# Expert tables of a large two-block layer stack: all first products ahead of the second, their results kept in DRAM, and the scatter groups set between them

## The chip, the cores and the metric

The kernel runs on one core of a Trainium2 chip. The metric is device time in microseconds from the start of the program to its end; lower is better. A core has five engines with a queue each: PE (TensorE, matmuls), ACT (ScalarE), DVE (VectorE), POOL (GpSimd) and SP (SyncE, which here only issues the loads of weights). They meet through semaphores. ACT and POOL issue some DMAs of their own.

## The reference, cut to what matters

A stack of two blocks over 256 tokens of width 1024. The change touches only the expert tables (`_peer`), which come twice, in layers 0 and 1 of the second block. A token picks 128 of 16384 experts, by product keys:

```python
q = (xt @ wq).reshape(T, PEER_HEADS, 2, PEER_DQ_HALF)
s1 = jnp.einsum('thd,nd->thn', q[:, :, 0], k1)
s2 = jnp.einsum('thd,nd->thn', q[:, :, 1], k2)
v1, i1 = lax.top_k(s1, PEER_TOPK)
v2, i2 = lax.top_k(s2, PEER_TOPK)
cand = (v1[..., :, None] + v2[..., None, :]).reshape(T, PEER_HEADS, PEER_TOPK * PEER_TOPK)
sc, pos = lax.top_k(cand, PEER_TOPK)
eidx = jnp.take_along_axis(cidx, pos, axis=-1).reshape(T, PEER_HK)
gate = jax.nn.softmax(sc.astype(jnp.float32), axis=-1)
...
act = jax.nn.gelu(jnp.einsum('td,tkd->tk', xb, ub), approximate=False)
return jnp.einsum('tk,tkd->td', gb * act, vb)
```

## The kernel before, in words

The kernel doesn't gather experts. It computes the first product of every expert with every token (the table `peer_u`, 128 tiles of 128 experts, 512 KB each), applies Gelu, multiplies by a dense table of gates `Gt` (zero where an expert wasn't chosen), and runs the second product with all of `peer_v`, again 128 tiles. Two tiles make a **pair**: 64 pairs of first products (`pe_pair`) and 64 of second products (`down_step` twice), each into one PSUM bank or into four accumulators.

Weights come in float32 and are multiplied as a high and a low part in fp32r, three matmuls for one. The two parts are made on the way: SP loads a tile into one of 3 raw buffers, ACT copies a half tile to its high part (L478), and DVE or POOL subtracts to get the low part (L501). The halves stand in a ring of 5 (`NHALF`), so that a half's place is free once PE has done the half five before it. A pair has four halves, numbered on through the program. Every engine's program calls `fed(n)` once its part of the work has used n more tiles, and splits then, in order, every half that may be split by that count:

```python
def splittable(self, m, tiles):
    if m == len(self.halves) or self.ready[self.halves[m][0]] > tiles:
        return False
    return self.freed[m] < 0 or self.halves[self.freed[m]][0] < tiles
```

Here `freed[m]` is half m - 5. `fed(2)` of pair p is called ahead of waiting for the pair's product, and counts its two tiles as used. The instructions that it writes wait, on ACT, for PE to be done with half m - 5, and on DVE and POOL for ACT's high part. Which of DVE and POOL makes the low part is written in the stream of loads (`stream_order`, `lo=`).

The gates come from the **choice** (`dve_choice`, on DVE, once for each 128 tokens: top 16 of 256 sums for 8 heads, indices, differences; `act_choice` takes Exp on ACT; then the softmax's end, three transposes on PE and a copy). The choice's results become `Gt` in the **scatter**, by groups of four tokens: for each two tokens DVE or POOL compares an iota with the second index (`p.b`: DVE for tokens 0 and 1 of a group, L95; POOL for tokens 2 and 3, L100), DVE compares with the first and multiplies by the gate (`p.a`, L100, one operation a token), PE multiplies the two for each token (128x128, fp32), and ACT copies four tokens' result to `Gt` (L155). The factors stand in three buffers of two tokens each.

The order is written out by hand, alike on all engines: 16 query tiles with their top 16; pairs 0 to 9; choice 0; scatter of tokens 0 to 127; pairs 10 to 17; choice 1; scatter of tokens 128 to 255; then a mixed run, in which first products 18 to 63 and second products of all pairs alternate. The Gelu results of pairs 0 to 17 are spilled to DRAM (`act_early`, four buffers) and read back on POOL's queue into three buffers `hb`; those of the later pairs go straight into `hb`. In the mixed run DVE multiplies `hb` by the gates (1.05 us at 512 elements, `p.hg`), ACT takes the high part (`p.hh`) and DVE the low part (`p.hl`), for PE's second product. The spill's four buffers lie in `arena`, the second products' left factors in `hid`.

Of the kernel before, what the change touches and what calls it, by code (L numbers as in the profile page):

```python
# [24 lines left out]
NSPILL = 18  # L25
# [179 lines left out]
def stream_order(dram):  # L205
# [27 lines left out]
    def peer(layer):  # L233
        for i in range(16):
            put(dram["wq"][layer, i])
        for i in range(2 * NSPILL):
            put(dram["peer_u"][layer, i])
        for k, n in steps(64, 3):
            i = turns()[n]
            if k == 0 and i >= NSPILL:  # L240
                for j in range(2):
                    put(dram["peer_u"][layer, 2 * i + j], lo="dve")
            elif k == 2:
                for j in range(2):
                    put(dram["peer_v"][layer, 2 * i + j], lo="dve")
# [42 lines left out]
def turns():  # L288
    return [x for i in range(NSPILL) for x in (i, NSPILL + i)] + list(range(2 * NSPILL, 64))


class Shared:


    def __init__(self, nc, ctx, dram, out):
# [27 lines left out]
        self.spill = nc.dram_tensor("spill", (2, NSPILL, 128, 512), F32)  # L323
# [1928 lines left out]
class Peer:  # L2252
    def __init__(self, S, layer):
# [16 lines left out]
        self.sel = R.get(3, 128)  # L2270
        self.gs = R.get(16)
        self.kT2 = R.get(2, 128)
        self.rb = [R.get(512) for _ in range(4)]
# [6 lines left out]
        self.turns = turns()  # L2280
        self.norm_in, self.norm_out = 5 + 2 * layer, 6 + 2 * layer

    def pe(self, pe):
# [23 lines left out]
        for k, i in steps(64, 3):  # L2307
            if k == 0:
                if self.turns[i] >= NSPILL:
                    self.pe_pair(pe, self.turns[i])  # L2310
            elif k == 2:
                h = self.hs[i % 2]
                pe.wait_ge(S.acted, "p.hh", n, i)
                pe.wait_ge(S.vdone, "p.hl", n, i)
                for j in range(2):
                    pe.down_step(lambda t: (h[:, 256 * j + 128 * t:256 * j + 128 * t + 128],
                                            h[:, 512 + 256 * j + 128 * t:640 + 256 * j + 128 * t]),
                                 (i, j) == (0, 0), (i, j) == (63, 1))
                S.product.at["p.down", n, i] = S.product.n
# [9 lines left out]
    def pe_choice(self, pe, t):  # L2329
        S, n = self.S, self.layer  # L2330
        b = pe.open("p.c", n, t)
        pe.wait_ge(S.vdone, "p.sel", n, t)
        for a in range(3):
            ins = pe.tr(b[:, 128 * a:128 * a + 128], self.sel[:, a, :])
        pe.out(ins, ("p.c", n, t))
# [12 lines left out]
    def act(self, act):  # L2348
# [10 lines left out]
        for i in range(10):  # L2359
            self.act_early(act, i)  # L2360
        self.act_choice(act, 0)
        for t0 in range(0, 128, 4):
            self.act_scatter(act, t0)
        for i in range(10, NSPILL):
            self.act_early(act, i)
        self.act_choice(act, 1)
        act.wait_ge(S.vdone, "p.iT", n, 1)
        for i in range(4):
            act.wait_ge(S.load(f"spill{n}_{i}"), "spill", NSPILL - 1 - (NSPILL - 1 - i) % 4)
        for t0 in range(128, 256, 4):  # L2370
            self.act_scatter(act, t0)
        for k, i in steps(64, 3):
            if k == 0:
                p = self.turns[i]
                if p >= NSPILL:
                    act.fed(2)
                    act.wait_ge(S.product, "p.u", n, p)
                    if i >= 3:
                        act.wait_ge(S.vdone, "p.hl", n, i - 3)
                    act.act(self.hb[i % 3], S.bank["p.u", n, p], ACT.Gelu, ("p.ge", n, i), ("drained", ("p.u", n, p)))  # L2380
            elif k == 1:
# [12 lines left out]
    def act_early(self, act, i):  # L2394
        S, n = self.S, self.layer
        r = self.rb[i % 4]
        ring = S.load(f"spill{n}_{i % 4}")
        act.fed(2)
        act.wait_ge(S.product, "p.u", n, i)
        if i >= 4:  # L2400
            act.wait_ge(ring, "spill", i - 4)
# [4 lines left out]
    def act_choice(self, act, t):  # L2406
        S, n = self.S, self.layer
        g3 = self.sel[:, 2, :].rearrange("p (h k) -> p h k", h=8)
        act.wait_ge(S.vdone, "p.g", n, t)
        act.act(g3, g3, ACT.Exp, ("p.g", n, t))  # L2410

# [6 lines left out]
    def dve(self, dve):  # L2418
# [12 lines left out]
        dve.fed(20)  # L2431
        self.dve_choice(dve, 0)
        for t0 in range(0, 128, 4):
            self.dve_scatter(dve, t0)
        dve.fed(2 * NSPILL - 20)
        self.dve_choice(dve, 1)
        for t0 in range(128, 256, 4):
            self.dve_scatter(dve, t0)
        for k, i in steps(64, 3):
            if k == 0:  # L2440
                p = self.turns[i]
                r3 = self.hb[i % 3].rearrange("p (i t) -> p i t", i=2)
                g = self.Gt[:, :, 2 * p:2 * p + 2].rearrange("p t i -> p i t")
                if p < NSPILL:
                    dve.wait_ge(S.load(f"back{n}_{i % 3}"), "back", i)
                else:
                    dve.fed(2)
                    dve.wait_ge(S.acted, "p.ge", n, i)
                dve.wait_ge(S.acted, "p.G", n, 252)
                dve.tt(r3, r3, g, ALU.mult, ("p.hg", n, i))  # L2450
# [30 lines left out]
    def dve_choice(self, dve, t):  # L2481
        S, n = self.S, self.layer
        iota16 = S.C["iota"][:, 0:16]
        VV, II, IIf, SC, PP, oh, sel, gs = self.VV[t], self.II[t], self.IIf, self.SC, self.PP, self.oh, self.sel, self.gs
# [20 lines left out]
        dve.tt(g3, SC, bc(SC[:, :, 0], 2, 16), ALU.subtract, ("p.g", n, t))  # L2505
        dve.wait_ge(S.acted, "p.g", n, t)
# [3 lines left out]
        dve.wait_ge(S.product, "p.c", n, t)  # L2510
        dve.cp(self.iT[:, :, 128 * t:128 * t + 128], S.bank["p.c", n, t][:, 0:384].rearrange("p (a t) -> p a t", a=3),
               ("p.iT", n, t), ("drained", ("p.c", n, t)))

    def dve_scatter(self, dve, t0):
        S, n = self.S, self.layer
        iota, iT = S.C["iota"], self.iT
        for tp in (0, 2):
            m = t0 + tp
            ab = self.AB[m // 2 % 3]
            dve.wait_ge(dve.done, "p.iT", n, t0 // 128)  # L2520
# [9 lines left out]
    def pool(self, pool):  # L2530
        S, n = self.S, self.layer
        pool.fed(16 + 20)
        for t0 in range(0, 128, 4):
            self.pool_scatter(pool, t0)
        pool.fed(2 * NSPILL - 20)
        for t0 in range(128, 256, 4):
            self.pool_scatter(pool, t0)
        for k, i in steps(64, 3):
            if k == 0:
                p = self.turns[i]  # L2540
                if p < NSPILL:
                    pool.wait_ge(S.load(f"spill{n}_{p % 4}"), "spill", p)
                    if i >= 3:
                        pool.wait_ge(S.vdone, "p.hl", n, i - 3)
                    else:
                        pool.wait_ge(S.acted, "p.G", n, 252)
# [5 lines left out]
            elif k == 2:  # L2552
                pool.fed(2)
# [229 lines left out]
```

## Time and profile before

| | us |
|---|---|
| median of 3 runs | 3538.53 (3537.34 to 3541.25) |
| the profiled execution | 3538.66 |
| its span, first to last instruction | 3536.7 |
| PE busy | 3163.5 (89% of the span) |
| DVE busy | 2315.6 (65%) |
| ACT busy | 1856.4 (52%) |
| POOL busy | 813.2 (23%) |
| mean granted TensorE clock | 0.925 |

Busy time is summed over an engine's instructions; it doesn't tell whether the engine was waited for. The granted clock is 1.00 at 2.4 GHz and 0.50 at 1.2 GHz. The two expert-table stages run from about 1465 to 2397 us and from about 2591 us to the end.

### The profile page before, as it was taken

What the parts mean: (1) busy time and instruction counts of PE and PEld (TensorE: products, weight loads), DVE (VectorE), ACT (ScalarE), POOL (GpSimd) and SP (SyncE); (2) the same over time, 40 slices, a digit from 0 to 9 for tenths busy, and PEclk for the clock granted to TensorE, in tenths of its full rate; (3) what the DMA queues carried; (4) which work ended last, traced back from release to release, by engine and by line L of the source; (5) the groups of instructions that cost most, each with busy time, mean ns of one, the idle gap of its engine ahead of it and who ended that gap; (6) DMA issues with size and microseconds to landing.
All of it is one profiled execution on the core that took longest, in us unless ns stands there. A gap on an engine that the chain in (4) does not pass through costs nothing.

```text
span 3536.7 us, 48626 instructions
## 1 busy us (share of the span) xinstructions
PE 3163.5 (89%) x17902; PEld 2733.0 (77%) x17902; DVE 2315.6 (65%) x4081; ACT 1856.4 (52%) x2816; POOL 813.2 (23%) x770
## 2 busy tenths in 40 slices
PE   7769999887999968889499999997798769999998
PEld 6658888656788856788488899996588758889997
DVE  0558998125899946585966666664668486666666
ACT  4447887334688834444255555554344425555554
POOL 6230000412100024588410000004368640000000
PEclk8879999788999978899799999997799979999999
DMA  5238998343799922363056666663244306666665
GB/s 184 60 125 311 370 369 325 111 143 123 275 371 371 370 69 89 117 189 91 29 163 205 211 190 188 187 186 127 64 151 149 120 20 196 210 201 190 188 188 166
DMA packets 183198, 653.75 MB, mean 185 GB/s; under 512 B 20689, under 2 KB 21073, under 8 KB 182547
## 3 DMA queue, kind: packets, MB, share of 16 engines
q1 hardware_dynamic: 170784, 617.69, 52.5%
q10 hardware_dynamic: 7476, 17.24, 1.4%
q0 software_dynamic: 4704, 15.73, 1.2%
q8 instruction: 144, 2.36, 0.3%
q14 instruction: 90, 0.74, 0.1%
HBM read 635.89 MB, written 14.68 MB: 184 GB/s over the span
## 4 chain that ended last, share of the span: by engine, by line
PE 82%; DVE 9%; ACT 3%; POOL 2%; DMA 2%; issue 1%; ACTq 0%; DVEq 0%; SPq 0%; POOLq 0%
PE ps L549 81%; DVE arena L95 3%; POOL splitb L501 2%; PE ps L560 2%; DVE hrow L105 1%; DVE arena L105 1%; ACT arena L155 1%; DMA rawb<-in_peer_u 1%; ACT splitb L478 1%; ACT L155 1%; DVE arena L100 1%; DVE arena L150 0%; DMA rawb<-in_cmp_w 0%; DVE arena L115 0%; DVE arena L145 0%
## 5 line engine op out<-in xcount | busy, mean ns | idle before, releaser
L478 ACT ACTIVATE splitb<-rawb 128x512 fp32r<-128x512 f32 x1328 | 833.7, 630 | 1006.9 <-PE ps L549 900.5
L549 PE MATMUL ps<-hH,splitb 128*128 128x256 f32 x5248 | 982.6, 286 | 7.3 <-POOL splitb L501 7.0
L501 POOL TENSOR_TENSOR splitb<-rawb,splitb 128x512 fp32r<-128x512 f32 x448 | 598.5, 1349 | 1605.0 <-ACT splitb L478 1595.0
L501 DVE TENSOR_TENSOR splitb<-rawb,splitb 128x512 fp32r<-128x512 f32 x880 | 596.7, 691 | 499.2 <-ACT splitb L478 498.8
L549 PEld LDWEIGHTS ps<-hH,splitb 128*128 128x128 f32 x5248 | 839.3, 194 | 14.7 <-issue 4.4
L549 PE MATMUL ps<-splitb,hid 128*128 128x512 f32 x3444 | 810.7, 392 | 9.2 <-ACT hid L155 9.2
L549 PEld LDWEIGHTS ps<-splitb,hid 128*128 128x128 f32 x3444 | 644.5, 189 | 141.1 <-ACT hid L155 9.6
L549 PE MATMUL ps<-hL,splitb 128*128 128x256 f32 x2624 | 749.1, 285 | 0.0
L549 PEld LDWEIGHTS ps<-hL,splitb 128*128 128x128 f32 x2624 | 510.4, 195 | 3.5
L549 PE MATMUL ps<-experts_r 128*128 128x512 f32 (+1 forms) x1348 | 332.1, 397 | 15.3 <-ACT experts_r L155 9.0
L549 PEld LDWEIGHTS ps<-experts_r 128*128 128x128 f32 x1348 | 253.7, 194 | 70.6 <-ACT experts_r L155 7.5
L155 ACT ACTIVATE arena<-ps 128x512 f32<-128x512 f32 (+4 forms) x328 | 173.5, 529 | 199.7 <-PE ps L549 181.2
L501 DVE TENSOR_TENSOR splitb<-experts,splitb 128x1024 fp32r<-128x1024 f32 x188 | 228.1, 1224 | 17.1 <-ACT splitb L478 13.5
L478 ACT ACTIVATE splitb<-experts 128x1024 fp32r<-128x1024 f32 x192 | 202.0, 1060 | 46.2 <-PE ps L549 46.0
L549 PE MATMUL ps<-splitb,hH 128*128 128x512 f32 x640 | 215.9, 420 | 10.3 <-ACT arena L155 9.6
L549 PE MATMUL ps<-arena 128*128 128x128 f32 (+8 forms) x896 | 179.5, 353 | 37.8 <-ACT arena L155 14.4
L549 PE MATMUL ps<-splitb,experts_r 128*128 128x512 f32 x780 | 196.1, 396 | 0.0
L549 PE MATMUL ps<-aux 128*128 128x128 f32 x1024 | 177.2, 310 | 20.9 <-DVE aux L100 6.0
L100 POOL TENSOR_SCALAR aux<-cst,aux 128x128 f32<-128x128 f32 x256 | 165.3, 656 | 126.5 <-DVE aux L111 99.6
L549 PEld LDWEIGHTS ps<-arena 128*128 128x128 f32 (+3 forms) x896 | 134.4, 227 | 77.2 <-issue 24.6
L549 PEld LDWEIGHTS ps<-aux 128*128 128x128 f32 x1024 | 142.3, 205 | 56.7 <-issue 36.2
L501 DVE TENSOR_TENSOR experts_r<-experts,experts_r 128x1024 fp32r<-128x1024 f32 x140 | 169.8, 1224 | 22.4 <-ACT experts_r L478 17.5
(147 smaller groups left out, 3245.2 us busy)
## 6 DMA issues: line engine op xcount, KB each, us to landing
rawb<-in_peer_u SPq DMA_DIRECT2D x256, 512.0 KB, 4.1
rawb<-in_peer_v SPq DMA_DIRECT2D x256, 512.0 KB, 4.1
experts<-in_moe_gu SPq DMA_DIRECT2D x228, 512.0 KB, 5.4
experts<-in_moe_d SPq DMA_DIRECT2D x108, 512.0 KB, 5.3
rawb<-in_moe_gu SPq DMA_DIRECT2D x92, 512.0 KB, 5.4
rawb<-in_moe_d SPq DMA_DIRECT2D x52, 512.0 KB, 5.3
rawb<-in_wq SPq DMA_DIRECT2D x32, 512.0 KB, 3.6
spill<-arena ACTq DMA_DIRECT2D x36, 256.0 KB, 4.2
```

The source lines that it names most:

```text
L95: self.eng.tensor_tensor(o, a, b, op).then_inc(self.done.sem, self.done.step(*names))
L100: self.eng.tensor_scalar(o, a, s1, s2, op0, op1).then_inc(self.done.sem, self.done.step(*names))
L105: self.eng.scalar_tensor_tensor(out=o, in0=a, scalar=s, in1=b, op0=op0, op1=op1, accum_out=accum).then_inc(self.done.sem, self.done.step(* ...
L155: self.eng.activation(o, a, f, bias=bias, scale=scale).then_inc(self.done.sem, self.done.step(*names))
L478: self.eng.activation(S.split(m)[0], S.raw(n)[:, off:off + w], ACT.Copy).then_inc(S.hi.sem, S.hi.step(("half", m)))
L501: self.eng.tensor_tensor(l, raw, h.bitcast(F32), ALU.subtract).then_inc(self.low.sem, self.low.step(("half", m), *([("raw", n)] if last el ...
L549: return self.eng.matmul(o, w, x, start=start, stop=stop)
L560: return self.eng.transpose(o, a, self.S.ident)
```

## The change: what it does

All 64 first products run first and all are spilled, through two buffers that now lie in `gb` (the second half of `hid`'s place). Both choices stand on DVE ahead of its first `fed`, with the softmax's end parted off (`dve_gates`) and each with its own `sel`; ACT takes the Exps behind pairs 17 and 21 and copies the transposed choices (`act_places`) behind pair 22. The scatter's 64 groups follow pairs 23 to 58 (`groups(p)`), two behind 28 of them and one behind 8. Of the low parts of `peer_u`, POOL makes all up to pair 23 and those of odd pairs behind it, DVE those of even pairs from 24 on. The second products come last in one run, each reading its spilled result back. Nothing is computed differently.

```diff
+        for i in range(128):
+            put(dram["peer_u"][layer, i], lo="dve" if i // 2 >= SCATTER and i // 2 % 2 == 0 else "pool")
+        for i in range(128):
+            put(dram["peer_v"][layer, i], lo="dve")
...
+CHOICE = 22
+SCATTER, SCATTERED = 23, 59
+
+
+def groups(p):
+
+    first, last = (min(64, max(0, 64 * (i - SCATTER) // (SCATTERED - SCATTER))) for i in (p, p + 1))
+    return [4 * g for g in range(first, last)]
...
-        self.rb = [R.get(512) for _ in range(4)]
+        self.rb = [S.gb[:, 1024 + 512 * i:1536 + 512 * i] for i in range(2)]
...
     def pe(self, pe):
-        for i in range(10):
-            self.pe_pair(pe, i)
-        self.pe_choice(pe, 0)
-        for t0 in range(0, 128, 4):
-            self.pe_scatter(pe, t0)
-        for i in range(10, NSPILL):
-            self.pe_pair(pe, i)
-        self.pe_choice(pe, 1)
-        for t0 in range(128, 256, 4):
-            self.pe_scatter(pe, t0)
...
+        for p in range(64):
+            self.pe_pair(pe, p)
+            if p == CHOICE:
+                for t in range(2):
+                    self.pe_choice(pe, t)
+            for t0 in groups(p):
+                self.pe_scatter(pe, t0)
+        for i in range(64):
+            h = self.hs[i % 2]
+            pe.wait_ge(S.acted, "p.hh", n, i)
+            pe.wait_ge(S.vdone, "p.hl", n, i)
...
     def act(self, act):
+        for p in range(64):
+            self.act_early(act, p)
+            if p == CHOICE - 5:
+                self.act_choice(act, 0)
+            elif p == CHOICE - 1:
+                self.act_choice(act, 1)
+            elif p == CHOICE:
+                for t in range(2):
+                    self.act_places(act, t)
+            for t0 in groups(p):
+                self.act_scatter(act, t0)
+        for p, i in steps(64, 2):
+            if p == 0:
...
+                if i == 1:
+                    for k in range(2):
+                        act.wait_ge(S.load(f"spill{n}_{k}"), "spill", 62 + k)
...
     def dve(self, dve):
-        dve.fed(20)
-        self.dve_choice(dve, 0)
-        for t0 in range(0, 128, 4):
-            self.dve_scatter(dve, t0)
-        dve.fed(2 * NSPILL - 20)
-        self.dve_choice(dve, 1)
-        for t0 in range(128, 256, 4):
-            self.dve_scatter(dve, t0)
+        for t in range(2):
+            self.dve_choice(dve, t)
+        for t in range(2):
+            self.dve_gates(dve, t)
+        for p in range(64):
+            dve.fed(2)
+            for t0 in groups(p):
+                self.dve_scatter(dve, t0)
...
     def pool(self, pool):
+        pool.fed(16)
+        for p in range(64):
+            pool.fed(2)
+            for t0 in groups(p):
+                self.pool_scatter(pool, t0)
+        for i in range(64):
+            pool.wait_ge(S.load(f"spill{n}_{i % 2}"), "spill", i)
+            if i >= 3:
+                pool.wait_ge(S.vdone, "p.hl", n, i - 3)
+            else:
+                pool.wait_ge(S.acted, "p.G", n, 252)
+            ring = S.load(f"back{n}_{i % 3}")
+            pool.eng.dma_start(self.hb[i % 3], S.spill.ap()[n, i, :, :]).then_inc(ring.sem, ring.step(("back", i)))
+        pool.fed(128)
```

How it moves the instructions is seen in their order on DVE and POOL, the two engines that the scatter's matmuls wait for. On DVE before, in the scatter of layer 0 (`aux<-cst,aux` are the comparisons, 128x256 for two tokens' second index, 128x128 for one token's first index and gate), groups of four tokens follow each other with nothing between:

```order
L95 TENSOR_TENSOR aux<-cst,aux 128x256 [waits s_product]
L100 TENSOR_SCALAR aux<-cst,aux 128x128 x2
L100 TENSOR_SCALAR aux<-cst,aux 128x128 [waits s_product]
L100 TENSOR_SCALAR aux<-cst,aux 128x128
L95 TENSOR_TENSOR aux<-cst,aux 128x256 [waits s_product]
```

On DVE now, behind pairs 25 and 26 of layer 0 (`splitb<-rawb,splitb` are the low parts of halves, `s_hi` is ACT's high part):

```order
L500 TENSOR_TENSOR splitb<-rawb,splitb 128x512 [waits s_hi] x3
L94 TENSOR_TENSOR aux<-cst,aux 128x256 [waits s_product]
L99 TENSOR_SCALAR aux<-cst,aux 128x128 x2
L99 TENSOR_SCALAR aux<-cst,aux 128x128 [waits s_product]
L99 TENSOR_SCALAR aux<-cst,aux 128x128
L94 TENSOR_TENSOR aux<-cst,aux 128x256 [waits s_product]
L99 TENSOR_SCALAR aux<-cst,aux 128x128 x2
L99 TENSOR_SCALAR aux<-cst,aux 128x128 [waits s_product]
L99 TENSOR_SCALAR aux<-cst,aux 128x128
L500 TENSOR_TENSOR splitb<-rawb,splitb 128x512 [waits s_hi]
L94 TENSOR_TENSOR aux<-cst,aux 128x256 [waits s_product]
```

Three low parts (the last three halves of pair 26) stand ahead of the groups behind pair 25, and one (the first half of pair 28) ahead of those behind pair 26. On POOL before, a run of low parts ends with that of the first half of pair 11, and the comparisons for tokens 2 and 3 of each group of the first scatter follow:

```order
L501 TENSOR_TENSOR splitb<-rawb,splitb 128x512 [waits s_hi] x133
L100 TENSOR_SCALAR aux<-cst,aux 128x128 [waits s_vdone]
L100 TENSOR_SCALAR aux<-cst,aux 128x128
L100 TENSOR_SCALAR aux<-cst,aux 128x128 [waits s_product]
L100 TENSOR_SCALAR aux<-cst,aux 128x128
```

On POOL now, behind pairs further on in the same layer, one behind an odd pair first, and then an even one:

```order
L500 TENSOR_TENSOR splitb<-rawb,splitb 128x512 [waits s_hi]
L99 TENSOR_SCALAR aux<-cst,aux 128x128 [waits s_product]
L99 TENSOR_SCALAR aux<-cst,aux 128x128
L99 TENSOR_SCALAR aux<-cst,aux 128x128 [waits s_product]
L99 TENSOR_SCALAR aux<-cst,aux 128x128
L500 TENSOR_TENSOR splitb<-rawb,splitb 128x512 [waits s_hi] x3
L99 TENSOR_SCALAR aux<-cst,aux 128x128 [waits s_product]
L99 TENSOR_SCALAR aux<-cst,aux 128x128
```

POOL has the other parity: one low part ahead of the groups behind an odd pair, three ahead of those behind an even one.

## Rows read from the trace of the kernel before

**Rows 1.** The page, part 4: the chain that ended last, in shares.

```profile
PE 82%; DVE 9%; ACT 3%; POOL 2%; DMA 2%; issue 1%; ACTq 0%; DVEq 0%; SPq 0%; POOLq 0%
```

**Rows 2.** Layer 0, stretches: us, busy PE, PEld, DVE, ACT, POOL, clock, DMA, GB/s.

```profile
1522.22:1584.20 61.98, 58.48 (x483) 57.78 (x481) 57.07 (x143) 30.68 (x50) 56.62 (x37) 1.00 0.62 194
1584.20:1592.03 7.83, 0.90 (x5) 0.54 (x4) 2.22 (x7) 2.71 (x4) 4.86 (x5) 0.72 0.64 208
1592.03:1639.86 47.83, 43.89 (x257) 35.43 (x257) 46.84 (x158) 18.52 (x31) 40.71 (x64) 0.94 0.01 1
1639.86:1686.10 46.24, 46.24 (x387) 46.10 (x385) 2.75 (x4) 24.89 (x40) 34.65 (x27) 1.00 0.70 207
1686.10:1728.34 42.24, 0.94 (x4) 0.53 (x4) 38.36 (x86) 2.71 (x4) 0.82 (x2) 0.55 0.07 24
1728.34:1776.12 47.78, 43.84 (x256) 35.52 (x257) 46.80 (x158) 18.52 (x31) 40.49 (x64) 0.94 0.00 1
1776.12:1786.73 10.61, 6.00 (x52) 5.82 (x50) 5.25 (x8) 6.27 (x9) 1.15 (x2) 0.95 0.44 136
1786.73:2396.00 609.27, 609.27 (x3689) 547.93 (x3690) 394.36 (x556) 326.62 (x538) 8.62 (x16) 1.00 0.63 194
```

**Rows 3.** The same columns, layer 1, the wait for choice 1.

```profile
2812.61:2855.18 42.57, 0.88 (x4) 0.53 (x4) 38.34 (x85) 2.71 (x4) 0.81 (x2) 0.55 0.08 27
```

**Rows 4.** Timeline, PE: start, duration, form, count, idle before with its releaser.

```profile
1479.25 1.38 PE L549 MATMUL ps<-arena 128*128 128x128 f32 x10 [0.39 <-ACT arena L155]
...
1786.73 8.38 PE L549 MATMUL ps<-splitb,hid 128*128 128x512 f32 x24 [4.61 <-ACT hid L155]
```

**Rows 5.** Timeline, POOL: low halves, and comparisons of the scatter.

```profile
1531.98 31.40 POOL L501 TENSOR_TENSOR splitb<-rawb,splitb 128x512 fp32r<-128x512 f32 x23 [1.66 <-ACT splitb L478]
1563.88 24.37 POOL L501 TENSOR_TENSOR splitb<-rawb,splitb 128x512 fp32r<-128x512 f32 x13 [0.49 <-ACT splitb L478]
...
1638.04 1.29 POOL L100 TENSOR_SCALAR aux<-cst,aux 128x128 f32<-128x128 f32 x2 [0.19 <-PE ps L549]
```

**Rows 6.** Timeline: end of a pair on PE; ACT's splits; DVE's halves.

```profile
1781.83 0.28 PE L549 MATMUL ps<-hH,splitb 128*128 128x256 f32 x1
...
1782.21 0.63 ACT L478 ACTIVATE splitb<-rawb 128x512 fp32r<-128x512 f32 x1 [0.86 <-PE ps L549]
...
1798.08 0.63 ACT L478 ACTIVATE splitb<-rawb 128x512 fp32r<-128x512 f32 x1 [0.87 <-PE ps L549]
...
1781.58 2.49 DVE L501 TENSOR_TENSOR splitb<-rawb,splitb 128x512 fp32r<-128x512 f32 x4
1784.78 1.05 DVE L95 TENSOR_TENSOR aux<-aux,arena 128x512 f32<-128x512 f32 x1 [0.72 <-ACT aux L155]
...
1798.75 0.69 DVE L501 TENSOR_TENSOR splitb<-rawb,splitb 128x512 fp32r<-128x512 f32 x1 [0.81 <-ACT splitb L478]
```

**Rows 7.** Timeline, DVE and PE: first group of a scatter, and last.

```profile
1591.15 0.42 DVE L95 TENSOR_TENSOR aux<-cst,aux 128x256 f32<-128x256 f32 x1
...
1592.03 7.32 PE L549 MATMUL ps<-aux 128*128 128x128 f32 x36 [1.51 <-DVE aux L100]
...
1774.14 0.41 DVE L95 TENSOR_TENSOR aux<-cst,aux 128x256 f32<-128x256 f32 x1
...
1776.12 0.36 PE L549 MATMUL ps<-hH,splitb 128*128 128x256 f32 x1
```

**Rows 8.** Stretches, columns as in rows 2: the clock and PE.

```profile
1570.00:1584.00 14.00, 10.52 (x84) 10.21 (x84) 12.05 (x5) 4.55 (x8) 14.00 (x9) 1.00 0.51 160
...
1390.00:1393.00 3.00, 1.53 (x12) 1.18 (x10) 2.72 (x5) 0.70 (x2) 0.00 (x0) 1.00 0.33 134
1393.00:1400.00 7.00, 6.94 (x20) 5.33 (x20) 6.15 (x15) 0.63 (x1) 0.71 (x1) 0.51 0.01 2
...
1786.00:1792.00 6.00, 5.27 (x13) 4.14 (x14) 3.06 (x4) 1.12 (x2) 0.54 (x1) 0.50 0.30 105
```

**Rows 9.** The spill tensor's DMAs, issue to landing.

```profile
DMA to landing us min/median/max: 2.0/4.3/6.1
```

More of the change, by code:

```diff
@@ L24 @@
 EXPERT_ROOM = 1024 * XRAW + 2560
-NSPILL = 18
 AB_AUX = dict(conv=32, gateb=8, headg=512, rel=8, wif=64)
@@ L2269, in __init__ @@
         self.oh = R.get(8, 16, 16)
-        self.sel = R.get(3, 128)
+        self.sel = [R.get(3, 128) for _ in range(2)]
         self.gs = R.get(16)
         self.kT2 = R.get(2, 128)
-        self.rb = [R.get(512) for _ in range(4)]
+        self.rb = [S.gb[:, 1024 + 512 * i:1536 + 512 * i] for i in range(2)]
         self.iT = S.aux[:, 0:768].rearrange("p (a t) -> p a t", a=3)
@@ L2296, in pe @@
                 pe.out(ins, ("p.s", n, t, i0))
-        for i in range(10):
-            self.pe_pair(pe, i)
-        self.pe_choice(pe, 0)
-        for t0 in range(0, 128, 4):
-            self.pe_scatter(pe, t0)
-        for i in range(10, NSPILL):
-            self.pe_pair(pe, i)
-        self.pe_choice(pe, 1)
-        for t0 in range(128, 256, 4):
-            self.pe_scatter(pe, t0)
[L2307 to L2319, printed above, removed]
+        for p in range(64):
[9 more added lines that the diff above has]
+            pe.wait_ge(S.vdone, "p.hl", n, i)
+            for j in range(2):
+                pe.down_step(lambda t: (h[:, 256 * j + 128 * t:256 * j + 128 * t + 128],
+                                        h[:, 512 + 256 * j + 128 * t:640 + 256 * j + 128 * t]),
+                             (i, j) == (0, 0), (i, j) == (63, 1))
+            S.product.at["p.down", n, i] = S.product.n
         S.product.at["rows", self.norm_out] = S.product.n
@@ L2395, in act_early @@
         S, n = self.S, self.layer
-        r = self.rb[i % 4]
-        ring = S.load(f"spill{n}_{i % 4}")
+        r = self.rb[i % 2]
+        ring = S.load(f"spill{n}_{i % 2}")
         act.fed(2)
         act.wait_ge(S.product, "p.u", n, i)
-        if i >= 4:
-            act.wait_ge(ring, "spill", i - 4)
+        if i >= 2:
+            act.wait_ge(ring, "spill", i - 2)
         act.act(r, S.bank["p.u", n, i], ACT.Gelu, ("p.ue", n, i), ("drained", ("p.u", n, i)))
@@ L2407, in act_choice, with act_places @@
         S, n = self.S, self.layer
-        g3 = self.sel[:, 2, :].rearrange("p (h k) -> p h k", h=8)
+        g3 = self.sel[t][:, 2, :].rearrange("p (h k) -> p h k", h=8)
         act.wait_ge(S.vdone, "p.g", n, t)
         act.act(g3, g3, ACT.Exp, ("p.g", n, t))
+    def act_places(self, act, t):
+        S, n = self.S, self.layer
+        act.wait_ge(S.product, "p.c", n, t)
+        act.cp(self.iT[:, :, 128 * t:128 * t + 128], S.bank["p.c", n, t][:, 0:384].rearrange("p (a t) -> p a t", a=3),
+               ("p.iT", n, t), ("drained", ("p.c", n, t)))
     def act_scatter(self, act, t0):
@@ L2531, in pool @@
         S, n = self.S, self.layer
[L2532 to L2546, printed above, removed]
-                    ring = S.load(f"back{n}_{i % 3}")
-                    pool.eng.dma_start(self.hb[i % 3], S.spill.ap()[n, p, :, :]).then_inc(
-                        ring.sem, ring.step(("back", i)))
-                else:
-                    pool.fed(2)
-            elif k == 2:
-                pool.fed(2)
+        pool.fed(16)
[12 more added lines that the diff above has]
+        pool.fed(128)
     def pool_scatter(self, pool, t0):
```

64 lines of the change are left out of this document (10 added, 54 removed).

## The prediction, made before the changed kernel was run

> **What bounds the kernel now.** I read the chain that ended last first: PE holds 82% of it and DVE 9% [rows 1], so only work that PE does, or waits for, counts. Then I cut the expert-table stage of layer 0 into stretches [rows 2]. PE is busy throughout the long mixed stretch (609.27 of 609.27 us) and while it runs pairs 10 to 17 (46.24 of 46.24, so 5.78 us a pair); what it loses, it loses around the choices and the scatter. In order:
>
> - pairs 0 to 9: 61.98 us, 4.2 more than ten times 5.78;
> - the wait for choice 0: 7.83;
> - scatter of 128 tokens: 47.83, in which DVE is busy for 46.84 and sets the pace;
> - after pair 17 the wait for choice 1: 42.24, of which DVE works 38.36 and PE 0.94;
> - scatter again: 47.78;
> - one pair and a wait of 4.61 for the first down product: 10.61.
>
> Layer 1 repeats this (42.57 for the second wait) [rows 3], so I count every term twice.
>
> **What the change removes.** The two waits and the two solid scatter stretches: 7.83 + 47.83 + 42.24 + 47.78 = 145.7 us a layer. If nothing came back, that would be 291 us. The pairs and the down products remain: 64 of each, at 5.78 and, from the mixed stretch, (609.27 - 45 x 5.78 - 2.9 of slow clock) / 64 = 5.4 us.
>
> **What comes back, term 1: both choices under pairs.** Choice 0 already ran under pairs. While it did, POOL made 13 low halves in 24.37 us, 1.87 each, against 31.40/23 = 1.365 just before [rows 5]; PE eats one in 1.445. So 24.37 - 13 x 1.445 = 5.6 us of supply was lost, 4.2 of which PE felt, the rest lay in the buffers. Now a second full choice runs there with POOL still doing every low half, and POOL's margin of 0.08 a half refills almost nothing between them: 2 x 5.6 - 4.2 = 7.0 more a layer. Bounds: 4 (the same as now) to 12. By the rows POOL itself lost 24.37 - 13 x 1.365 = 6.6 us to the choice. The Trainium skill (SBUF — State Buffer, "Who interferes with whom") has a stricter rule: a DVE operation with two SBUF inputs blocks GpSimd's reads for the whole instruction. By it POOL would lose the full length of each such operation in a choice, more than the rows show; the measurement decides, and the sum keeps 7.0. Both choices' transposes stay on PE: three are the 0.94 us of PE's work in the wait [rows 2], six 1.9, or 1.8 at full clock.
>
> **Term 2: the scatter between pairs, and what stands ahead of it.** 64 groups of four tokens go behind pairs 23 to 58: two groups behind 28 of these 36 pairs, one behind 8, evenly over odd and even ones. A splitter's ring holds five halves, a pair has four. So the `fed(2)` of pair p runs up to the first half of pair p+2, and that half's buffer is freed only by the last matmul of pair p itself. `fed(2)` stands ahead of the groups on DVE and on POOL; the order shows it. Nothing for PE's scatter matmuls behind pair p can begin, on the engine that owns this fifth half, before pair p has ended. Let E be the moment at which PE could start its next matmul: 1781.83 + 0.12. ACT's split begins at 1782.21, E + 0.26; the low part begins 0.67 behind a split (1798.75 against 1798.08), at E + 0.93 [rows 6].
>
> *Behind an even pair* the fifth half is DVE's: 2.49/4 = 0.62 [rows 6], so its scatter starts at E + 1.55. The first matmul comes 0.88 later (1592.03 against 1591.15), a group takes 1.48 (47.78/32 = 1.49), and from the last group's start to the next pair it is 1.98 (1776.12 against 1774.14) [rows 7]. Two groups: 1.55 + 1.48 + 1.98 = 5.01 us until the next pair; one: 3.53.
>
> *Behind an odd pair* it is POOL's, 1.365 long: POOL is free at E + 2.30, and its two comparisons for tokens 2 and 3 take 1.29 [rows 5], to E + 3.59. PE waits for them in order, with tokens 4 to 7 behind; with 0.2 to the matmul and half a microsecond for two tokens, one group ends at 4.28; the second group's comparisons take 1.29 more, 5.57.
>
> Sum: 14 x 5.01 + 4 x 3.53 + 14 x 5.57 + 4 x 4.28 = 179.4 us a layer. PE's own part is small: ten records of the same matmul shape take 1.38 [rows 4], two records to a token, 0.28; eight tokens are 2.2 us. The rest of each 5 us is waiting, now paid 36 times. This is the step on which the forecast rests.
>
> **Term 3: the clock.** PE will be idle or thinly used for about 5 us after each pair. The granted clock fell to half after the 4.61 us wait: it was 0.50 over 1786 to 1792, and the first 24 down matmuls took 8.38 us instead of 5.4, 2.9 lost [rows 4, 8]. It also fell after 1390 to 1393, where PE was busy 1.53 of 3.00 us, and was 0.51 over the next seven. It held at 1.00 over 1570 to 1584, where gaps up to 1.62 us stood between dense halves (10.52 busy of 14.00) [rows 8]. The new stretches have 3 us of standing in 5, so I place them with the first two. A fall costs nothing while PE waits anyway; the part on dense matmuls costs. Bounds per stretch 0 and 2.9; I take 1.2, since the lower clock begins inside the wait and covers about half a pair of dense work. 36 x 1.2 = 43.2 a layer. The Trainium skill (TensorE: Matmul & The Clock Gate, "A second HAM failure mode: psum-queue depth-cycling") says that frequent short idles between groups of matmuls make the clock alternate. By that rule term 3 is paid everywhere; by the row of 1570 to 1584 it is nothing, and the sum would be 86 us less.
>
> **What I cost at nothing, and its cover.** 46 more spills a layer, written and read, 256 KB each: ACT's issue and Gelu fit in a pair (ACT is busy 24.89 of 46.24) [rows 2]; the two-buffer ring waits for the spill two pairs back, 11.5 us, and a spill's DMA lands in 4.3 us, 6.1 at most [rows 9]. Read back, three buffers give about 7.5 us between the freeing of one and its use, again against 4.3 plus 0.5 of issue; if it took over 8, every down pair would wait for it. Bytes: 1.25 MB per 5.4 us is 243 GB/s; at 207 the DMA engines are busy 0.70 of the time [rows 2], so about 0.82 then. ACT switches between Exp and Gelu four times a layer, for which no row here has a price; the halves are split five ahead, 7.2 us of cover. In the down run DVE has four low halves at 0.69, a multiplication at 1.05 and one more low part at 0.69 [rows 6], 4.5 us of work per 5.4. The first down product waits as now (4.61 and the slow clock behind): DVE must finish the fifth half, two multiplications and one low part behind pair 63; no change. ACT's wait for the last spills falls under down product 0.
>
> **Sum.** Per layer -145.7 + 7.0 + 1.8 + 179.4 + 43.2 = +85.7; twice +171. The profiled execution took 3538.66 us (span 3536.7), the median of the runs is 3538.53, so one base serves: 3710.
>
> **Rivals.**
>
> *A, the forecast:* waits and clock falls, 3710, chance 0.50.
>
> *B, waits only:* the clock holds, because dense pairs stand between: 3538.7 + 2 x 42.5 = 3624, chance 0.28. For it speaks the row of 1570 to 1584; against it the length of the standing.
>
> *C, the scatter hides (faster):* DVE and POOL prepare the tokens during the pair, so PE pays only 256 x 0.28 = 71 us: -145.7 + 71 + 8.8 = -66 a layer, 3407. For it: DVE is busy for only 2.75 of 46.24 us under pairs 10 to 17 [rows 2], so there is room for the 95 us of scatter. It decides if the 36 stretches average under (145.7 - 8.8)/36 = 3.8 us, clock included; mine are 5.0 and 1.2. Against it stand the in-order queues. Chance 0.11.
>
> *D, worse than A:* each fall costs the full 2.9: +104 instead of +43 a layer, 3832, chance 0.08. About no change (stretches of 3.8): 0.03.
>
> **How the numbers follow.** Predicted is A. The range 3590 to 3800 takes in B with its own spread (term 1 down to 4, stretches 0.3 shorter: 30 less) and A with clock losses up to 2.4; that holds 0.8. C and D lie outside. A measurement of this kernel tells about 0.2% (7 us) from no change; faster 0.11, within 0.03, slower 0.86.
>
> **What would show it.** Pairs 0 to 22 should run dense but for some 11 us of gaps that POOL ends. Choices end before pair 22, and the 42 us gap is gone. From pair 23 PE should stand after every pair: about 2.4 us until DVE's first token behind even ones, about 2 us in the middle of the first group behind odd ones, ended by POOL. The stage's stretches between pairs should average 5.0 us at full clock, about 6.2 with the falls. The granted clock should alternate there. The down run should be solid at 5.4 us. I am wrong if DVE's or POOL's scatter is found running before the pair ends (then C), or if the down run is starved by read-backs (above 8 us to land).

## The result, and the profile after

The changed kernel takes 3705.4 us (median of 4, 3698.2 to 3711.0) against 3537.9 (median of 4): 1.047 times the time before, 95% interval 1.045 to 1.049. The profiled execution took 3698.2 us. The forecast was 3710, in a range of 3590 to 3800. The page of the changed kernel (span; busy and share of it; PE's granted clock by slices; the chain, which answers to [rows 1]):

```profile
span 3696.3 us, 48810 instructions
PE 3236.9 (88%) x17902; PEld 2818.2 (76%) x17902; DVE 2211.8 (60%) x3869; ACT 1853.8 (50%) x2820; POOL 1161.1 (31%) x1070
...
PEclk9789998797999888998888899997899988889999
...
PE 79%; DVE 8%; POOL 6%; ACT 3%; DMA 2%; issue 2%; ACTq 0%; DVEq 0%; SPq 0%; POOLq 0%
```

POOL's share of the chain rose from 2% to 6%, and the clock row has 88888 and 8888 in the two places where groups stand between pairs. Layer 0 by stretches, in the columns of [rows 2]: pairs 0 to 22; the 36 stretches behind pairs 23 to 58 with the 35 pairs between them; pairs 59 to 63; the run of second products:

```profile
1522.18:1664.70 142.52, 134.04 (x1106) 132.81 (x1105) 103.68 (x226) 72.05 (x120) 132.01 (x89) 1.00 0.66 204
1671.26:2095.73 424.47, 330.68 (x2195) 317.29 (x2193) 157.28 (x392) 145.14 (x242) 182.33 (x200) 0.86 0.36 112
2095.73:2124.75 29.02, 29.02 (x243) 28.82 (x241) 7.62 (x11) 14.55 (x24) 11.95 (x11) 1.00 0.64 197
2129.20:2475.00 345.80, 345.80 (x1519) 286.11 (x1520) 268.90 (x376) 191.60 (x314) 32.80 (x61) 1.00 0.72 237
```

Only the second row loses time. With its 35 pairs at 5.78 it holds 424.5 - 202.3 = 222.2 us that isn't first products, where the forecast had 179.4 + 43.2 = 222.6; at a granted clock of 0.86. The two waits for a choice and the two blocks of scatter that the change removed are gone (145.7 a layer), and this stands in their place. The down run is solid, 345.8/64 = 5.40 us a pair.

Now PE in the middle of that row, behind pair 28 and then behind pair 29 (timeline of PE; start, duration, form, count, idle before and who ended it):

```profile
1729.83 0.28 PE L548 MATMUL ps<-hH,splitb 128*128 128x256 f32 x1
1732.32 1.20 PE L548 MATMUL ps<-aux 128*128 128x128 f32 x8 [2.21 <-DVE aux L99]
1733.73 2.01 PE L548 MATMUL ps<-aux 128*128 128x128 f32 x8 [0.22 <-DVE aux L99]
1735.39 0.56 PE L548 MATMUL ps<-hH,splitb 128*128 128x256 f32 x1
...
1742.87 0.68 PE L548 MATMUL ps<-aux 128*128 128x128 f32 x4 [0.70 <-DVE aux L99]
1745.82 1.99 PE L548 MATMUL ps<-aux 128*128 128x128 f32 x12 [2.27 <-POOL aux L99]
1747.46 0.56 PE L548 MATMUL ps<-hH,splitb 128*128 128x256 f32 x1
```

Behind the even pair PE stands 2.37 us from the moment at which it could go on (1729.95) to the first token; behind the odd one it gets two tokens, and then stands 2.27 for POOL. What DVE, POOL and ACT do at the same time, in the same columns:

```profile
1730.20 0.63 ACT L477 ACTIVATE splitb<-rawb 128x512 fp32r<-128x512 f32 x1 [0.86 <-PE ps L548]
...
1730.87 0.71 DVE L500 TENSOR_TENSOR splitb<-rawb,splitb 128x512 fp32r<-128x512 f32 x1 [9.83 <-ACT splitb L477]
1731.50 0.41 DVE L94 TENSOR_TENSOR aux<-cst,aux 128x256 f32<-128x256 f32 x1
...
1742.98 1.38 POOL L500 TENSOR_TENSOR splitb<-rawb,splitb 128x512 fp32r<-128x512 f32 x1 [8.66 <-ACT splitb L477]
1744.34 2.58 POOL L99 TENSOR_SCALAR aux<-cst,aux 128x128 f32<-128x128 f32 x4
```

DVE had been idle for 9.83 us, through the whole of pair 28, before a single low part whose high part ACT could make only behind the pair's end, and the scatter came behind it. POOL had been idle for 8.66 us, and its comparisons came behind the same kind of half.

### The profile page after: what moved, and what is told of

It reads as the page before. It is cut to its first block, busy times and chain, and to the rows that moved or that the text cites. A ratio compares the mean times of both kernels' runs of the same rounds, so it can differ in the third digit from the quotient of the medians.

```text
span 3696.3 us, 48810 instructions
## 1 busy us (share of the span) xinstructions
PE 3236.9 (88%) x17902; PEld 2818.2 (76%) x17902; DVE 2211.8 (60%) x3869; ACT 1853.8 (50%) x2820; POOL 1161.1 (31%) x1070
## 4 chain that ended last, share of the span: by engine, by line
PE 79%; DVE 8%; POOL 6%; ACT 3%; DMA 2%; issue 2%; ACTq 0%; DVEq 0%; SPq 0%; POOLq 0%
PE ps L548 77%; POOL splitb L500 5%; ACT splitb L477 2%; DVE arena L94 2%; PE ps L559 2%; POOL aux L99 1%; DVE hrow L104 1%; DVE arena L104 1%; DMA rawb<-in_peer_u 1%; DVE splitb L500 1%; ACT arena L154 1%; DVE arena L99 0%; DVE aux L99 0%; DVE aux L94 0%; DMA rawb<-in_cmp_w 0%
## 5 line engine op out<-in xcount | busy, mean ns | idle before, releaser
L500 POOL TENSOR_TENSOR splitb<-rawb,splitb 128x512 fp32r<-128x512 f32 x656 | 886.1, 1366 | 1759.0 <-ACT splitb L477 1747.2
L548 PE MATMUL ps<-hH,splitb 128*128 128x256 f32 x5248 | 1039.4, 297 | 17.4 <-POOL splitb L500 16.1
L548 PEld LDWEIGHTS ps<-hH,splitb 128*128 128x128 f32 x5248 | 885.0, 205 | 22.7 <-ACT splitb L477 13.8
L500 DVE TENSOR_TENSOR splitb<-rawb,splitb 128x512 fp32r<-128x512 f32 x672 | 454.6, 692 | 726.2 <-ACT splitb L477 725.8
L548 PE MATMUL ps<-hL,splitb 128*128 128x256 f32 x2624 | 772.3, 294 | 0.0
L548 PEld LDWEIGHTS ps<-hL,splitb 128*128 128x128 f32 x2624 | 537.7, 205 | 0.0
L548 PE MATMUL ps<-aux 128*128 128x128 f32 x1024 | 207.7, 364 | 186.9 <-DVE aux L99 109.2
L548 PEld LDWEIGHTS ps<-aux 128*128 128x128 f32 x1024 | 176.1, 253 | 213.6 <-POOL aux L99 88.8
L154 ACT ACTIVATE arena<-ps 128x512 f32<-128x512 f32 (+3 forms) x292 | 152.5, 522 | 345.4 <-PE ps L548 335.6
L2528 POOL DMA_DIRECT2D aux<-spill x128 | 68.9, 539 | 604.7 <-DVE hid L94 581.4
```

Source lines behind the costliest of these rows:

```text
L154: self.eng.activation(o, a, f, bias=bias, scale=scale).then_inc(self.done.sem, self.done.step(*names))
L500: self.eng.tensor_tensor(l, raw, h.bitcast(F32), ALU.subtract).then_inc(self.low.sem, self.low.step(("half", m), *([("raw", n)] if last el ...
L548: return self.eng.matmul(o, w, x, start=start, stop=stop)
L2528: pool.eng.dma_start(self.hb[i % 3], S.spill.ap()[n, i, :, :]).then_inc(ring.sem, ring.step(("back", i)))
```

## The experiments

Each kernel is the changed one with the edit shown. Times are medians in us; the kernel before took 3536 to 3538 beside them. "Region" is the window of layer 0 that holds the groups.

**1. The fifth half behind the groups (e1_hold1), the fourth and fifth (e2_hold2), three (e9_hold3).** A splitter can now stop short of what the count allows:

```diff
-    def fed(self, n=1):
+    def fed(self, n=1, hold=0):
         self.tile += n
-        self.split_to(self.tile)
+        last = self.half
+        while self.S.splittable(last, self.tile):
+            last += 1
+        while self.half < last - hold:
+            self.split_half(self.half)
+            self.half += 1
...
-            dve.fed(2)
+            dve.fed(2, hold=1 if groups(p) else 0)
...
-            pool.fed(2)
+            pool.fed(2, hold=1 if groups(p) else 0)
```

> The changed kernel, but behind pairs 23 to 58 DVE and POOL make the low part of the fifth half (4p+8) after the groups instead of ahead of them. Theory F (the fifth half, freed only by the pair's last matmul, stands ahead of the scatter): behind even pairs POOL's low part of half 4p+7 now ends last (about 0.75 us behind the pair), its comparisons 1.3 later, so two groups take about 4.2 us; behind odd pairs DVE is free about 0.1 behind the pair, two groups take about 3.6. Stretches sum to about 127 us a layer instead of 192, clock loss about halves: near 3550. Rival P (DVE and POOL slow each other, or PE pays for changing between the two kinds of matmul): the order of one half doesn't matter, within 20 us of 3705.

> As the one before, with the fourth and the fifth half (4p+7, 4p+8) both made after the groups. Theory F: both engines can prepare six tokens while the pair runs; PE goes on at once, two groups take about 2.9 us, one 1.3, together 92 us a layer; the clock stays at 1.00 there, and the 45 us a layer of clock loss go too: 3705 - 2 x (225 - 92) = 3440, below the kernel before. Rival P: within 20 us of 3705. Rival C (the clock falls anyway since the scatter's matmuls are thin): stretches shrink but pairs stay at 6.7 us, near 3500.

> The pair-by-pair run with three halves made after the groups instead of two (3457.5 us). Theory F: with two held back nothing of the halves is in the way any more; what is left in a double stretch (2.84 and 3.41 us) is the ring of three factor buffers, which this doesn't touch: within 10 us of 3457. Rival H (more holding back goes on helping): under 3440; if the late halves instead come too late for the next pair: over 3480.

Measured: 3529.7 with one half held back (0.998 of the kernel before, 0.997 to 0.999), 3457.5 with two (0.978, 0.976 to 0.980), 3455.5 with three (0.977, 0.975 to 0.978). Against the expectations the first is 20 us faster, the second 18 slower. The same instructions in another order are worth 248 us. The regions with one and with two:

```profile
1671.49:2010.20 338.71, 287.00 (x2194) 272.96 (x2193) 167.65 (x392) 145.46 (x243) 174.35 (x200) 0.97 0.46 141
```

```profile
1665.82:1966.74 300.92, 271.05 (x2195) 262.27 (x2193) 161.38 (x391) 144.77 (x242) 187.34 (x198) 1.00 0.50 157
```

From 424.5 to 338.7 to 300.9, and the clock from 0.86 to 0.97 to 1.00. Theory F holds, and rival P, that the order doesn't matter, falls; so does C, that the clock falls anyway. With two held back, PE goes on at once with three quarters of a double stretch and then waits for POOL, whose comparisons wait for PE to be done with a factor buffer (PE's timeline in that kernel, then POOL's):

```profile
1784.25 1.52 PE L553 MATMUL ps<-aux 128*128 128x128 f32 x12
1787.19 0.71 PE L553 MATMUL ps<-aux 128*128 128x128 f32 x4 [1.42 <-POOL aux L99]
...
1784.95 2.18 POOL L99 TENSOR_SCALAR aux<-cst,aux 128x128 f32<-128x128 f32 x2 [4.21 <-PE ps L553]
```

The ring of factor buffers isn't all of this wait. The two comparisons of POOL in that window (ns: shortest, median, longest) took 0.66 and 1.54 us. During the second, from 1785.65 to 1786.66, DVE subtracted a half and then compared for two tokens; in the changed kernel, with no such operation of DVE beside them, the last three of POOL's four comparisons above took 0.60 each.

```profile
L99 POOL TENSOR_SCALAR aux<-cst,aux x2: 662/1100/1537, 1785.0 to 1785.6; 128x128 f32<-128x128 f32 x2
```

The third half held back changes nothing (2.0 us, inside the spread of both). That fits a wait that the halves' order doesn't touch, but it doesn't part the ring from the slowed comparison.

**2. All groups in one block (e3_solid).**

```diff
-    first, last = (min(64, max(0, 64 * (i - SCATTER) // (SCATTERED - SCATTER))) for i in (p, p + 1))
-    return [4 * g for g in range(first, last)]
+    return [4 * g for g in range(64)] if p == 63 else []
```

> The changed kernel with all 64 groups in one block behind pair 63 instead of between pairs; low parts are made by the same engines as in the changed kernel. Theory F: nothing stands between groups, so 256 tokens take twice 47.8 us as before the change plus 2 to 3 us at the start, and pairs 23 to 63 run dense: 225 us of stretches and slow pairs a layer become about 99, near 3455. Rival S (the spills, the read-backs or both choices under pairs are what costs): they are all still there, so the time stays above 3650.

Measured: 3457.6 (0.978, 0.976 to 0.979). The spills, the read-backs, both choices under pairs and the owners of the low parts are all still in it, and it is 248 us faster than the changed kernel. So none of those is what costs: rival S falls. PE's timeline has one wait at the block's start, and a longer one at its end than before the change:

```profile
1901.98 5.36 PE L547 MATMUL ps<-aux 128*128 128x128 f32 x28 [2.59 <-DVE aux L99]
...
1910.43 86.42 PE L547 MATMUL ps<-aux 128*128 128x128 f32 x468 [0.21 <-POOL aux L99]
2004.09 6.29 PE L547 MATMUL ps<-splitb,hid 128*128 128x512 f32 x17 [7.25 <-ACT hid L154]
```

**3. PE's waits filled with matmuls (e4_filler).** The product that they write is overwritten by the tokens' own; the result is unchanged.

```diff
         b = pe.open("p.G", n, t0)
+        p = next(q for q in range(64) if t0 in groups(q))
         for tp in (0, 2):
             ab = self.AB[(t0 + tp) // 2 % 3]
+            fill = {(0, 0): 17, (1, 0): 6, (1, 2): 16}.get((p % 2, tp), 0) if t0 == groups(p)[0] else 0
+            for k in range(fill):
+                pe.mm(b[:, 128 * tp:128 * tp + 256], S.hH[:, k % 8, 0:128], S.hH[:, k % 8, :], True, True)
```

> The changed kernel with matmuls added whose result is overwritten: 17 of 256 columns (about 2.0 us) ahead of the first token behind even pairs, 6 ahead of the first and 16 ahead of the third behind odd pairs, to fill PE's waits and nothing else. Clock theory (term 3: low clock costs about 45 us a layer): the granted clock stays at 1.00 in the region, pairs go from 6.7 back to 5.8 us and the tokens speed up: about 3615 to 3635. Rival N (the clock costs nothing, what is lost is waiting alone): 3705 or a little more, since more matmuls are issued.

Measured: 3625.7 (1.026, 1.024 to 1.027), 79.7 us faster with some 700 more matmuls a layer. A stretch of 6 us on PE in the changed kernel (start and end, length, busy time and records of PE, granted clock, DMA share, GB/s) and two dense matmuls in it, then both here, then the whole region with all engines, in the columns of [rows 2]:

```profile
1746.00:1752.00 6.00, 6.00 (x37) 0.72 0.01 3
...
1748.03 0.63 PE L548 MATMUL ps<-hH,splitb 128*128 128x256 f32 x2
```

```profile
1746.00:1752.00 6.00, 5.60 (x45) 1.00 0.34 125
...
1750.22 0.40 PE L548 MATMUL ps<-hH,splitb 128*128 128x256 f32 x2
```

```profile
1678.15:2060.14 381.99, 366.22 (x2896) 349.96 (x2895) 157.86 (x392) 145.55 (x243) 182.03 (x200) 1.00 0.41 125
```

The changed kernel had PE busy for the whole of these 6 us with 37 records, this one gets through 45. The two stretches don't hold the same mix of matmuls; the dense ones by themselves took 0.63 us for two behind the group, and take 0.40 at full clock. The region at clock 1.00 is 382.0: less 35 x 5.78, 179.7 us of waits and tokens, where term 2 said 179.4. The rest, 424.5 - 382.0 = 42.5, is the clock, where term 3 said 43.2. Rival N falls, and the split of the loss into waiting and clock is measured.

**4. One group a tile (e5_tile), and the same without holding back (e8_tile_nohold).** Groups behind each of the tiles 46 to 109, counts tile by tile, on ACT too:

```diff
+def group_of(q):
+    return [4 * (q - 46)] if 46 <= q < 110 else []
...
             for j in range(2):
                 pe.proj(b[:, 256 * j:256 * j + 256], ("p.u", n, p))
+                for t0 in group_of(2 * p + j):
+                    self.pe_scatter(pe, t0)
...
-        for p in range(64):
-            dve.fed(2)
-            for t0 in groups(p):
+        for q in range(128):
+            dve.fed(1, hold=2 if group_of(q) else 0)
+            for t0 in group_of(q):
                 self.dve_scatter(dve, t0)
```

> Built on the run that makes the fourth and fifth half after the groups (3457.5 us): one group behind each of the 64 tiles of pairs 23 to 54 instead of two behind most pairs, splitting counted tile by tile, the last two halves that a count allows made after the group. There a double group takes 2.84 or 3.41 us and a single one 0.80 or 1.07, since tokens 6 and 7 wait for a factor buffer (three buffers of two tokens). Theory F: every stretch is a single one with its four tokens ready: 64 x 0.8 to 1.1 = 51 to 70 us a layer against 96.7, so 3404 to 3365 less nothing: about 3390. Rival Q (POOL, with 1.365 a half and 1.29 a group, becomes the bound in odd pairs: 4.0 us a tile against 3.8): 3430 to 3460.

> The tile-by-tile run (3374.8 us) with only its order of halves undone: every half that the count allows is made ahead of the group. Theory F: each of the 64 groups a layer waits again for a half that the tile just done has freed; where DVE owns it a single group takes 3.5 us, where POOL owns it 4.3, 250 us a layer instead of 52 at full clock, and with one wait for every 2.9 us of dense work the clock is low for much of the region: from 3770 (no clock loss) to 3950, likely 3850, slower than the changed kernel. Rival G (what made that run fast is the single groups, and the order of halves is worth little): under 3500.

Measured: 3374.8 with the hold (0.955, 0.954 to 0.956), 15 below the expectation and the best kernel here, 163 us faster than before the change and 331 faster than the changed kernel. Without the hold, 3911.5 (1.106, 1.104 to 1.109): in this arrangement 537 us hang on where up to two halves stand in two queues. Rival G falls. Rival Q falls too: POOL keeps up. The region with the hold, PE's timeline in it, and then two waits without the hold:

```profile
1670.42:1907.69 237.27, 237.27 (x2019) 237.27 (x2018) 170.67 (x378) 132.22 (x221) 177.82 (x190) 1.00 0.55 175
```

```profile
1741.16 1.05 PE L558 MATMUL ps<-aux 128*128 128x128 f32 x8
1744.92 1.05 PE L558 MATMUL ps<-aux 128*128 128x128 f32 x8
```

```profile
1803.94 0.71 PE L558 MATMUL ps<-aux 128*128 128x128 f32 x4 [2.27 <-POOL aux L99]
1812.29 1.22 PE L558 MATMUL ps<-aux 128*128 128x128 f32 x4 [2.83 <-POOL aux L99]
```

With the hold PE is busy for all 237.27 us from behind the first group on, a tile and its group come every 3.76 us (1744.92 - 1741.16), and a group costs 3.76 - 2.89 = 0.87 us, 0.22 a token. Without it the expectation of 3850 was 61 us short; it had left 40 us a layer for the clock. Over the whole region of layer 0 the granted clock is 0.80:

```profile
1664.44:2175.10 510.66, 345.44 (x2025) 330.74 (x2025) 147.98 (x384) 134.70 (x225) 166.28 (x192) 0.80 0.26 83
```

Less 63 tiles at 2.89, that leaves 328.6 us, 79 more than the 250 expected at full clock. The slower clock is the likely place of it; no run fills these waits to show it.

**5. All low parts on DVE (e6_dvelow).**

```diff
-            put(dram["peer_u"][layer, i], lo="dve" if i // 2 >= SCATTER and i // 2 % 2 == 0 else "pool")
+            put(dram["peer_u"][layer, i], lo="dve" if i // 2 > SCATTER else "pool")
```

> The changed kernel with the low parts of all pairs from 24 on made by DVE, POOL keeping only its comparisons. Theory F: the fifth half is DVE's behind every pair, so every stretch is like those behind even ones: first token after 2.37 us, never a wait for POOL in the middle; at full clock 28 x 5.01 + 8 x 3.53 = 168.5 instead of 179.4 us a layer, clock losses about as before: 3680 to 3690, still far above 3538. Rival P (POOL and DVE on one port is what slows the region): without POOL's subtractions the stretches fall well under 4 us, and the time comes near 3600.

Measured: 3637.7 (1.028, 1.027 to 1.030). Both expectations missed it, theory F's by 42 to 52 us and rival P's by 38. The waits came as theory F has them, also behind the odd pair 29 (the second row of PE's timeline; behind it the region in the columns of [rows 2]):

```profile
1735.92 1.20 PE L548 MATMUL ps<-aux 128*128 128x128 f32 x8 [2.19 <-DVE aux L99]
1746.63 1.20 PE L548 MATMUL ps<-aux 128*128 128x128 f32 x8 [2.19 <-DVE aux L99]
```

```profile
1676.90:2067.89 390.99, 305.44 (x2194) 291.18 (x2193) 188.67 (x462) 144.16 (x240) 76.02 (x126) 0.93 0.37 122
```

The region at 391.0 holds 188.7 us beside its pairs against 222.2. Term 2's change of owner accounts for 179.4 - 168.5 = 10.9 of the 33.5; the clock, 0.93 against 0.86, goes with the rest. What I had wrong was "clock losses about as before": with one wait of 2.35 us behind every pair and then tokens without a gap, the clock mostly holds. It isn't the odd pairs' wait in the middle alone that brings it down in the changed kernel. There a stretch and the pair behind it had the same clock behind pair 28 and behind pair 29:

```profile
1730.11:1742.17 12.06, 9.63 (x64) 9.30 (x64) 5.67 (x15) 4.21 (x7) 3.42 (x5) 0.86 0.35 107
1742.17:1754.94 12.77, 9.80 (x65) 9.25 (x64) 3.70 (x10) 4.21 (x7) 7.21 (x8) 0.87 0.31 92
```

Which property of the gaps costs the clock is open. Rival P's 3600 isn't reached: the waits are as long as F says, though POOL makes no low parts there. Its reason, that the two engines slow each other, is seen, but not on the path that PE waits for (last section).

**6. The second choice's four large lookups left out (e7_nohot).** The second 128 tokens get wrong experts.

```diff
+            if t == 0:
-            dve.tt(oh, bc(pf, 3, 16), i16, ALU.is_equal)
-            dve.tt(oh, oh, bc(i4[:, :, side, :], 2, 16), ALU.mult)
+                dve.tt(oh, bc(pf, 3, 16), i16, ALU.is_equal)
+                dve.tt(oh, oh, bc(i4[:, :, side, :], 2, 16), ALU.mult)
```

> The changed kernel with the four 128x2048 comparisons and multiplications of the second choice left out (its one-hot lookup isn't computed, so the second 128 tokens get wrong experts). Term 1: pairs 0 to 22 took 142.5 us, 9.6 more than 23 x 5.78; these four operations slow POOL's low parts, so the second cluster of gaps (4.5 us ending near 1626) mostly goes and the stretch takes about 138 us. Rival: the gaps come from the loads of tiles, and stay at 142.

PE's longest gaps within pairs 0 to 22 of the changed kernel come in two clusters, one for each choice:

```profile
1577.37 0.36 PE L548 MATMUL ps<-hH,splitb 128*128 128x256 f32 x1 [1.23 <-POOL splitb L500]
1580.64 0.35 PE L548 MATMUL ps<-hH,splitb 128*128 128x256 f32 x1 [1.60 <-POOL splitb L500]
...
1616.86 0.36 PE L548 MATMUL ps<-hH,splitb 128*128 128x256 f32 x1 [1.62 <-POOL splitb L500]
1622.63 0.35 PE L548 MATMUL ps<-hH,splitb 128*128 128x256 f32 x1 [1.22 <-POOL splitb L500]
1625.91 0.36 PE L548 MATMUL ps<-hH,splitb 128*128 128x256 f32 x1 [1.62 <-POOL splitb L500]
```

Without the four operations the first cluster stands and the second is gone; pairs 0 to 22 take 137.8 us instead of 142.5, where about 138 was expected. The whole program took 3691.2 us, 7.0 less than the profiled execution of the changed kernel (one execution each):

```profile
1523.82:1661.62 137.80, 133.50 (x1108) 132.80 (x1107) 92.33 (x222) 72.35 (x120) 124.51 (x89) 1.00 0.67 214
```

So the gaps are POOL's low parts slowed by these operations on DVE, not late loads. Two of these operations in the changed kernel (DVE's timeline), and POOL's six low parts around the four (ns: shortest, median, longest):

```profile
1609.99 2.29 DVE L94 TENSOR_TENSOR arena<-arena,cst 128x2048 f32<-128x2048 f32 x1
1612.32 3.27 DVE L94 TENSOR_TENSOR arena<-arena 128x2048 f32<-128x2048 f32 x1
...
L500 POOL TENSOR_TENSOR splitb<-rawb,splitb x6: 1289/3200/3319, 1610.3 to 1622.5; 128x512 fp32r<-128x512 f32 x6
```

Four of the six took 3.1 to 3.3 us and two 1.29, so each of the four lost about 2.0; and of DVE's operations three took 3.2 to 3.4 instead of 2.29. The Trainium skill (SBUF — State Buffer, "Who interferes with whom") names the pair, DVE operations with two SBUF inputs against GpSimd's reads, and calls it an exclusive lock. The trace agrees: each engine loses nearly the other's whole operation (2.0 of 2.29 us, 1.0 of 1.29).

## Why the prediction was right, step by step

- **Removed, 145.7 us a layer.** Right: no wait for a choice is left, and no solid block of scatter.
- **Term 1, both choices under pairs, +7.0.** Pairs 0 to 22 lost 142.5 - 23 x 5.78 = 9.6; with the 4.2 of before taken off, +5.4. The place and the cause are shown by experiment 6. The prediction took the loss as an average of 6.6 us a choice and read it as milder than one engine blocking the other for a whole operation; taken one by one, the low parts that meet such an operation do lose nearly all of it. Transposes: 1.8 forecast; 1671.26 - 1664.70 less a pair of 5.78 leaves 0.8.
- **Term 2, waits between pairs, +179.4.** Right to 0.3 us at full clock (179.7 in experiment 3), and by its parts: there the stretch behind pair 28 is 4.91 us (1738.59 - 1733.68) and the one behind pair 29 is 5.47 (1749.90 - 1744.43), against 5.01 and 5.57 forecast. PE's first token came 2.37 us behind an even pair (2.43 forecast). The cause, a half that the pair itself frees standing ahead of the groups on DVE and on POOL, is shown from both sides: holding halves back removes it (experiment 1), splitting finer without holding back multiplies it (experiment 4).
- **Term 3, the clock, +43.2.** 42.5 in the trace, 39.9 a layer by the medians ((3705.4 - 3625.7)/2). The size was chosen between bounds of 0 and 2.9 a stretch, so that it fits this closely is partly luck; experiment 5 shows that I did not know which shape of gap brings the clock down. The Trainium skill's sentence on short idles between groups of matmuls (TensorE: Matmul & The Clock Gate, "A second HAM failure mode: psum-queue depth-cycling") fits the changed kernel, where the granted clock alternates: 0.60 over 1733 to 1737 us, 0.98 over the next four.
- **Costed at nothing.** The 128 spills and read-backs didn't show: the down run is solid at 5.40 us a pair, and a DMA of the spill tensor lands in 4.2 us, 6.4 at most:

```profile
DMA to landing us min/median/max: 2.0/4.2/6.4
```

  The prediction's estimate of the DMA engines' load was too high: they were busy for 0.72 of the down run, not 0.82.

- **Missed, small.** The first down product waited 4.45 us, much as before (4.61), and the clock fell behind it again:

```profile
2129.20:2135.00 5.80, 5.80 (x19) 4.59 (x20) 2.92 (x4) 1.89 (x3) 1.08 (x2) 0.71 0.43 127
```

  At 0.71 over 5.8 us that is an estimate of 1.7 us lost, less than the 2.9 that I left in place. Even with it the whole down run took 345.8, which is 64 x 5.40, so nothing shows on top of the forecast's price of a pair. I count -2.9 for that and -0.2 for the shorter wait. With this -3.1 and the two smaller terms the layer comes to -145.7 + 5.4 + 0.8 + 222.2 - 3.1 = +79.6, twice 159, as the profiled executions have it (3698.2 - 3538.7 = 159.5).
- **Rivals.** B (waits alone, 3624) is what experiment 3 made by filling the waits: 3626. C (the scatter hides, 3407) is what the change becomes when the halves are held back: 3457.5 with groups by pairs, 3374.8 by tiles. C's price of a token was too high, 0.28 us against 0.22 measured back to back.

## What to carry to other kernels

- Where a ring is one deeper than what a step uses, the last refill of a step waits for that step's own end. Anything that is written behind this refill in an in-order queue starts only then. Put the refill last, behind the work that the next engine needs at once.
- "The engine is idle enough" is no argument for hiding work under another engine's: DVE idled for 9.83 us and still came late. Ask what stands ahead of the work in its queue and what releases that.
- When a wait recurs in short, even steps on PE, price the clock beside it, and fill the wait with throwaway matmuls to measure how much is clock.

## What was unexpected in the hardware

POOL's subtraction of a half also holds up DVE's small comparisons, which read one tensor only. Of the four 128x128 comparisons of DVE behind pair 29 of the changed kernel (ns: shortest, median, longest) one took 1.29 us instead of 0.34. It began at 1743.15, while POOL subtracted from 1742.98 on for 1.38, and ended 0.1 behind it. Below it stand all 256 comparisons of DVE in the region, in the changed kernel and then in experiment 5, where POOL subtracts nothing there:

```profile
L99 DVE TENSOR_SCALAR aux<-cst,aux x4: 341/343/1292, 1742.4 to 1743.2; 128x128 f32<-128x128 f32 x4
...
L99 DVE TENSOR_SCALAR aux<-cst,aux x256: 330/336/1292, 1673.4 to 2094.1; 128x128 f32<-128x128 f32 x128
...
L99 DVE TENSOR_SCALAR aux<-cst,aux x256: 333/342/466, 1679.6 to 2066.7; 128x128 f32<-128x128 f32 x128
```

In the changed kernel this happens once behind each of the 18 odd pairs, and without POOL's subtractions never. Here it hardly cost anything, since POOL's own comparisons came later still.

And the clock answers to how the gaps lie, not to their sum alone. Over the region PE was idle for 93.8 us in the changed kernel (424.47 - 330.68) at a clock of 0.86, and for 85.6 in experiment 5 (390.99 - 305.44) at 0.93: a tenth less idle time, and half the fall.
